# Value products of the odd layer placed between the last transposes of the even layer

## The reference

```
even:  h = h + concatenate([y_a, y_b], axis=-1) @ w_out_e
odd:   p = rmsnorm(h, norm_g[1]) @ w_in_o        # u, v, gate parts
       y = spatial_gating(gelu(u), gelu(v), ln_g, ln_b, sg_w, sg_b)
rmsnorm(x, g) = x * rsqrt(mean(x * x) + 1e-6) * g
spatial_gating: v is layer-normed over its 1024 channels, then mixed within
       chunks of 128 tokens by a masked 128 x 128 matrix per group
```

## Time and profile before

| | us |
|---|---|
| three runs | 4198.1, 4195.02, 7965.85 |
| median | 4198.1 |
| span of the profiled execution, first to last instruction | 4192.4 |
| own time of the profiled execution | not listed; the median less the span is 5.7 |
| mean granted TensorE clock | 0.983 of full speed |

### The profile page before, as it was taken

The page is one execution under the profiler, slowest core; times in us unless marked ns, Lnnn a source line. Parts: engine busy times, 40 slices in busy tenths (PEclk is TensorE's granted clock), DMA queues, the critical chain, the costliest instruction groups (busy, mean ns, idle before and its releaser), DMA issues.

```text
span 4192.4 us, 59831 instructions
## 1 busy us (share of the span) xinstructions
PE 3986.3 (95%) x26464; PEld 3236.2 (77%) x26464; DVE 1736.8 (41%) x2696; ACT 1318.4 (31%) x2201; POOL 1196.5 (29%) x613
## 2 busy tenths in 40 slices
PE   8899999999999999899999889999999999999998
PEld 4757676665998898677587777897888988888887
DVE  2545454533340257762314463332186432323353
ACT  3232323232232243562212353222275312121133
POOL 1202010112114355662232102343102532233354
PEclk9999999999999999999999999999999999999999
DMA  3101010003111121001011100130100211111111
GB/s 90 32 2 32 2 32 3 17 11 107 41 41 41 51 71 50 26 25 36 28 52 42 40 1 23 48 114 21 50 1 31 71 45 47 51 51 51 50 41 41
DMA packets 164979, 168.71 MB, mean 40 GB/s; under 512 B 8176, under 2 KB 152432, under 8 KB 164720
## 3 DMA queue, kind: packets, MB, share of 16 engines
q1 hardware_dynamic: 164720, 164.89, 12.3%
HBM read 156.48 MB, written 8.39 MB: 39 GB/s over the span
## 4 chain that ended last, share of the span: by engine, by line
PE 79%; DVE 10%; ACT 5%; POOL 3%; issue 3%; DMA 0%; POOLq 0%; SPq 0%; DVEq 0%; ACTq 0%
PE pair L635 16%; PE pair L637 16%; PE pair L636 16%; PE pair L600 9%; PE pair L623 3%; PE pair L611 2%; PE pair L1124 1%; PE pair L590 1%; PE pair L1314 1%; PE pair L785 1%; POOL H L3428 1%; PE pair L1284 1%; ACT BIG L2051 1%; PE pair L777 1%; POOL W_r L3370 1%
## 5 line engine op out<-in xcount | busy, mean ns | idle before, releaser
L635 PE MATMUL pair<-XT_r,W_r 128*128 128x512 f32 x1744 | 693.8, 398 | 8.3 <-ACT BIG L1989 1.9
L636 PE MATMUL pair<-BIG_r,W_r 128*128 128x512 f32 x1624 | 632.2, 389 | 0.0
L3370 POOL TENSOR_TENSOR W_r<-W,W_r 128x2048 fp32r<-128x2048 f32 (+1 forms) x74 | 326.8, 4416 | 753.9 <-ACT W_r L1452 753.9
L637 PE MATMUL pair<-XT_r,W_r 128*128 128x512 f32 x1232 | 480.0, 390 | 0.0
L635 PE MATMUL pair<-W_r,BIG_r 128*128 128x256 f32 (+1 forms) x1280 | 417.9, 327 | 1.9 <-POOL W_r L3370 0.8
L600 PE MATMUL pair<-XT,W 128*128 128x512 f32 x928 | 405.5, 596 | 3.1 <-POOL MIX L3243 2.2
L635 PEld LDWEIGHTS pair<-XT_r,W_r 128*128 128x128 f32 x1744 | 327.5, 188 | 85.0 <-issue 10.6
L637 PE MATMUL pair<-W_r,BIG_r 128*128 128x256 f32 (+1 forms) x1152 | 380.4, 330 | 0.0
L636 PEld LDWEIGHTS pair<-BIG_r,W_r 128*128 128x128 f32 x1624 | 305.0, 188 | 68.9 <-issue 6.7
L600 PEld LDWEIGHTS pair<-XT,W 128*128 128x128 f32 x928 | 175.1, 191 | 220.1 <-issue 218.6
L637 PE MATMUL pair<-W_r,MIX_r 128*128 128x256 f32 x960 | 271.6, 283 | 0.0
(11 more groups left out here) (437 smaller groups left out, 7804.5 us busy)
## 6 DMA issues: line engine op xcount, KB each, us to landing
W<-w_in SPq DMA_DIRECT2D x29, 1024.0 KB, 5.5
W<-w_in_e SPq DMA_DIRECT2D x33, 512.0 KB, 6.5
MIX<-w_up SPq DMA_DIRECT2D x15, 1024.0 KB, 5.3
MIX<-w_down SPq DMA_DIRECT2D x15, 1024.0 KB, 4.9
W<-w_in_o SPq DMA_DIRECT2D x12, 1024.0 KB, 5.1
W<-w_in SPq DMA_DIRECT2D x17, 512.0 KB, 4.2
H<-x SPq DMA_DIRECT2D x16, 512.0 KB, 9.4
W<-w_out SPq DMA_DIRECT2D x7, 1024.0 KB, 5.3
```

The source lines that it names most:

```text
L635: E.matmul(b[:, 0:n], lh, rh, start=k == ks[0], stop=False)
L636: E.matmul(b[:, 0:n], lh, rl, start=False, stop=False)
L637: mm = E.matmul(b[:, 0:n], ll, rh, start=False, stop=k == ks[-1])
L3370: G.tensor_tensor(WLO[k % 2][:, 0:n], WSTAGE[k % 2][:, 0:n], WHI[k % 2][:, 0:n], ALU.subtract).then_inc(*s_split.mark("split", k))
```

## The change

A third row buffer is taken in a free part of BIG, and the square of tile t waits for the transposes of tile t - 3. The transposes, the rounding copies and the differences of a tile stand one step later in their programs. The first `ODD_EARLY` = 4 value products, (0, 0) to (0, 3), follow the even layer's last product on TensorE, each behind a wait for its own tile's XL, so that the transposes of tiles 4 to 7 come out one behind each of them. ScalarE reads them out inside the even layer's steps, one step after the last. The 45 dummies before the transposes of tiles 5 to 7 go. The split of chunk 5 on ScalarE moves ahead of the first remaining value.

```
-        for st_, ts in (("even", {5: 15, 6: 15, 7: 5}), ("odd", {2: 7, 3: 4, 4: 15}), ("merged", {4: 14}),
+        for st_, ts in (("odd", {2: 7, 3: 4, 4: 15}), ("merged", {4: 14}),
-                {("even", "out", 0, 0): 10, ("even", "tr", 5, 0): 3, ("even", "tr", 6, 0): 3, ("even", "tr", 7, 0): 4},
+                {("even", "out", 0, 0): 10},
+        XN_E = [*XN_O, BIG[:, 17408:18432]]
+        ODD_EARLY = 4
...
+                for n, t in OUT_ORDER[:ODD_EARLY]:
+                    pe.wait_ge(*done("ev", "even", "tr", t, 1))
+                    pe_odd_value(n, t)
+                    yield None
-            follow(products(), pe_rms_tile(even, XN_O, 3))
+            follow(products(), pe_rms_tile(even, XN_E, 4))
+        def pe_odd_value(n, t):
+            ts = slice(t * P, (t + 1) * P)
+            pe_split_N(odd, "v", n, t, ODD_V + n, lambda k: (XH[:, k, ts], XL[:, k, ts]), KD)
...
-                for n, t in OUT_ORDER:
+                for n, t in OUT_ORDER[ODD_EARLY:]:
+                    pe_odd_value(n, t)
...
-                if t > 1:
-                    act.wait_ge(*done(st.name, "tr", t - 2, 1))
-                S.activation(xn[t % 2], H[:, t, :], ACT.Square, accum_out=SS[:, t:t + 1]).then_inc(
+                if t > 2:
+                    act.wait_ge(*done(st.name, "tr", t - 3, 1))
+                S.activation(xn[t % 3], H[:, t, :], ACT.Square, accum_out=SS[:, t:t + 1]).then_inc(
...
-                yield from nothing(3)
+                yield from nothing(4)
...
+                if st is even:
+                    yield None
+                    for n, t in OUT_ORDER[:ODD_EARLY]:
+                        act_odd_value(n, t)
+                        yield None
+        def act_odd_value(n, t):
+            act.wait_ge(*done("odd", "v", n, t))
+            S.activation(VN_O[:, t, n * Q:(n + 1) * Q], every.bank("odd", "v", n, t)[:, 0:Q],
+                         ACT.Gelu_apprx_tanh).then_inc(*odd.act.mark("ev", "odd", "v", n, t))
...
+            act_high(ODD_V + 1)
-                    if (n < 3 and t == 1) or (n, t) == (3, 4):
+                    if (0 < n < 3 and t == 1) or (n, t) == (3, 4):
                         act_high(ODD_V + n + 1)
...
-                V.scalar_tensor_tensor(xn[t % 2], H[:, t, :], RS[:, t:t + 1], row, ALU.mult, ALU.mult).then_inc(
+                V.scalar_tensor_tensor(xn[t % 3], H[:, t, :], RS[:, t:t + 1], row, ALU.mult, ALU.mult).then_inc(
-                yield from nothing(2)
+                yield from nothing(3)
...
-            follow((t if n == 3 else None for n, t in OUT_ORDER), mixed)
+            follow((t if n == 3 else None for n, t in OUT_ORDER[ODD_EARLY:]), mixed)
```

More of the change, by code:

```diff
@@ L935, in values @@
             def values():
-                for n, t in OUT_ORDER:
-                    ts = slice(t * P, (t + 1) * P)
-                    pe_split_N(odd, "v", n, t, ODD_V + n, lambda k: (XH[:, k, ts], XL[:, k, ts]), KD)
+                for n, t in OUT_ORDER[ODD_EARLY:]:
+                    pe_odd_value(n, t)
                     yield t if n == 3 else None
@@ L1759, in act_even @@
             high_part(*pieces[7])
-            act_out(even, EVEN_OUT, act_split_rms_tile(even, lambda t: done("even", "added", t), XN_O))
+            act_out(even, EVEN_OUT, act_split_rms_tile(even, lambda t: done("even", "added", t), XN_E))
         def act_out(st, first, tile):
@@ L1790, in act_odd @@
             act_copy_out(odd, every, ("sg_tr", 0), od["SGT"][:, 0:HALF], HALF)
+            act_high(ODD_V + 1)
             def values():
-                for n, t in OUT_ORDER:
-                    if (n < 3 and t == 1) or (n, t) == (3, 4):
+                for n, t in OUT_ORDER[ODD_EARLY:]:
+                    if (0 < n < 3 and t == 1) or (n, t) == (3, 4):
                         act_high(ODD_V + n + 1)
-                    act.wait_ge(*done("odd", "v", n, t))
-                    S.activation(VN_O[:, t, n * Q:(n + 1) * Q], every.bank("odd", "v", n, t)[:, 0:Q],
-                                 ACT.Gelu_apprx_tanh).then_inc(*odd.act.mark("ev", "odd", "v", n, t))
+                    act_odd_value(n, t)
                     yield t if n == 3 else None
@@ L2734, in dve_even @@
                         *even.dve.mark("even", "low", ct, half))
-            follow(dve_out(even, "h_again"), dve_split_rms_tile(even, XN_O, od["norm"]))
+            follow(dve_out(even, "h_again"), dve_split_rms_tile(even, XN_E, od["norm"]))
         def dve_odd():
```

## The result

| | before | changed |
|---|---|---|
| median, first comparison | 4196.6 us | 4176.5 us |
| range of its executions | 4193.6 to 4198.1 | 4173.1 to 4182.6 |
| span of the profiled execution | 4192.4 us | 4171.3 us |

The forecast was 4185.7 us, in a range of 4179 to 4194.

What follows compares the result with a forecast made beforehand. TensorE, busy 95% of 4192.4 us, was taken as the bound, with 15.2 us of dummies and idle at the even layer's end. Gains of 1.3 and 11.1 us made 12.4: 4198.1 - 12.4 = 4185.7 us, range 4179 to 4194.

Steps and rivals of the forecast that it cites:

- the sum: Even layer's end into odd layer: 12.4 us gained, 1.3 from later transposes, 11.1 from moved value products and the entry.
- the waits of tiles 1 to 3: Even layer: their transposes stop waiting for VectorE's normed row, 3 x 0.44 = 1.3 us gained.
- the cadence: TensorE after the last even product: one value product and one tile's transposes every 3.75 us.
- The wait of value 3: TensorE before value product 3: a new wait of 0.5 us for VectorE's difference of tile 4.
- From transposes 7 to TensorE's going on: Odd layer's entry: VectorE's queued differences of tiles 5 to 7 let TensorE go on 3.2 us after transposes 7 start.
- Chunk 4: Weights of the early value products: GpSimd's split, at an unchanged place, done by 1115.1 us, 4.5 us early.
- (a): Early values: slower ScalarE queue makes TensorE wait at values 1 to 3 and transposes 7; gain 7.4, 4190.7 us; chance 0.10.
- (b): Odd layer's entry: the waits move there whole; gain only 6.8 us, 4191.3 us; chance 0.06.
- (d): Value product 8: chunk 5's split comes late, making the kernel slower, 4208 us if it ends at 1173.5; chance 0.02.
- (c): Last gap, after transposes 7: clock falls without dummies; gain 10.7 or 9.0, 4187.4 to 4189.1 us; chance 0.12.
- The 5.7 us: Whole kernel: the median of 4198.1 us stands 5.7 us above the profiled span of 4192.4 us.
- the clock stayed at 1.00: Odd layer's entry: no clock fall after a 1.78 us idle gap before, so none expected after about 2 us.

Runs made afterwards that it cites:

- padded: The changed kernel with 56 more dummies (112 passes, 13.0 us) at the odd layer's entry; 4197.5 us, ratio 1.0000 to the kernel before.
- six values: The changed kernel with six early value products instead of four, 6 dummies gone and chunk 5 split earlier; 4176.8 us, again 4178.3 us.

## Why the prediction was right and wrong

**Right: the mechanism, and its size in the profiled pair.** The boundary gained 12.88 us, where the sum said 12.4. By its parts: the waits of tiles 1 to 3 went, 1.4 us (value 0 follows 31.54 us behind the square of tile 0, where the transposes of tile 4 had followed 32.94 behind it) for 1.3, and the cadence of 3.74 us stands for 3.75. The wait of value 3 came at its place and for its cause, VectorE's difference of tile 4, at a cost of 0.44 us for 0.5. From transposes 7 to TensorE's going on it took 2.81 us (1127.05 to 1129.86) for 3.2: the last normed row was done 1.05 us ahead of transposes 7, where I had 0.8, and the three differences behind it took 3.68 us for 3.75. The table was loaded once, and between the end of the root (1121.11) and the Gelu lie 1.31 us: the trace agrees again with the load of 1.28 us that the Trainium skill states (page "ScalarE: Activation LUTs", section "What ACT_TABLE_LOAD costs") and shows no drain of 1.38 us behind it. Chunk 4 was split 5.0 us early (1107.48 against value 0 at 1112.45), where 4.5 were chained. Rivals (a), (b) and (d) did not occur, and (c) in none of the profiles with early values.

**Wrong: the boundary's gain was taken for the whole gain.** This is the step that failed: "The profiled execution would have a span of 4192.4 - 12.4 = 4180.0 us; the median stands 5.7 above the span, so 4198.1 - 12.4 = 4185.7 us". It puts at nothing all that differs outside the boundary, and all by which the profiled execution differs from the usual one. The means of all executions are 4197.9 us before (76 executions, standard error 0.6) and 4177.8 changed (23, 0.9): 20.1 us less, 14.2 of them in the boundary and 5.9 outside it. The baseline of 4198.1 was good. The 5.7 us were a warning: in the changed kernel the profiled execution took 4173.06 us with a span of 4171.34, 1.7 us more; by the same 1.7 us, an estimate, the profiled execution of before took 4194.1, some 4 us less than the median that it was set against.

**Wrong as a part of that: the profiled boundary of before was taken for the usual one.** The step "the clock stayed at 1.00" over the gap of 1.78 us held in that execution. In the other five profiles of before the clock falls there and costs 1.5 to 1.6 us. In nine profiles with early values and the same gap (six changed, three padded) it did not fall, nor in that of three rows alone, with a gap of 1.87 us. So the boundary gained 14.2 us on average (79.99 to 65.82), 1.8 more than the sum. What holds the clock there in the one and not in the other was not tried.

**Wrong: the range.** Its step was "the two undisturbed runs of before differ by 3.1 us, and this scatter is on both medians". The 3.1 us were then counted once, and from 4183.1 and 4191.3 they give 4180.0 to 4194.4, not 4193. The 76 executions of before lie between 4186.7 and 4207.4 us with a standard deviation of 5.1 us, and the 23 of the changed kernel between 4171.1 and 4185.7 with 4.2. A median of three or four of them is good to 2 to 3 us, an estimate from these deviations. Two runs that happened to agree said nothing of that. But scatter alone did not make the miss: the mean of 23 executions is below the range as well. Nor is 2% "about what a measurement of this kernel can tell from no change": the interval of the first comparison is 0.25% wide.

**Open: the rest of 5.9 us.** It is over five times the standard error of the difference, 1.1 us, and the gain in the means is some 18 us or more in each of the four groups of runs with several executions, so chance among executions is an unlikely cause. The profiles put it mostly ahead of the edit. Of the six of each kernel, the boundary gives 14.2, the part behind 1.9 (3016.2 and 3014.3), and the part ahead 6.6 (1089.5 and 1082.9), 22.7 together. The last two are within what one program does between executions: 3013 to 3018, and 1083 to 1094 for before; the falls of the clock make that spread. Other kernels show such a rest too. By the means of their executions, and against the boundary's mean of 79.99 us, three rows alone gained 7.7 us with 3.8 in the boundary, the early values with two rows 15.0 with 10.2; six values gained 19.6 with 17.6, and the padded kernel lost 0.4 where its boundary is 1.7 shorter. So the rest is not tied to the moved values. No run shows a cause in the program ahead of its own edit, and none excludes one. The part of the 20 us that is shown to be the change's is 13 to 14 us.

## What to carry to other kernels

Where a stage ends in a tail of short dependent steps, the next stage's products whose own tile is ready can stand between them; what they gain is the tail's filler and idle time, and that was forecast to half a microsecond from durations in the trace, for an execution whose clock does what it did in that trace. A single profile doesn't say whether that is the usual case: here it was not, and the boundary gained 1.8 us more on average. Dummies that keep a clock up mark such a tail: they count as busy, so look for them by line. Cut a small effect out of the profile between two fixed instructions, since the total can scatter by as much as the effect; and take the scatter of the total from many executions before giving a range. Do not equate the gain of one stretch with the gain of the total before reading several profiles of the kernel as it is.

## What the runs showed of the hardware

- Up to the edit, identical code took from 1079.7 to 1094.0 us in 20 profiles. The difference is in stretches at a granted clock below 1, such as 0.76 against 1.00 from 138 to 152 us.
- Behind the same idle gap of 1.77 us the clock fell in five of six profiles of before (in one of them 0.72 in the stretch from 1131 to 1137 us), and in none of nine of the changed and padded kernels.
- Idle waits of 4.4 us in place of dummies brought the clock to 0.60 of full speed over 18 us, and a pair of transposes to 1.97 us instead of 1.09.
- One program against itself, 11 executions against 22, gave a ratio of 0.9991 with an interval that ends at 0.9999.
